# The first two tiles in quarters, half of the ple tiles two output tiles earlier, channel sums by halves and taps moved between heads, in a two-layer retention and convolution trunk on one core

## The reference

```python
for i in range(DEPTH):                       # DEPTH = 2, D_MODEL = 2048
    hn = _rms_norm(x, g_pre[i])
    q, k, v, g_r, a, b, g_c = jnp.split(hn @ w_in[i], SPLITS, axis=-1)    # 7 parts of 1024 columns
    # group A: rotary q, k; retention over 8 heads x 128; norm over each head; * silu(g_r)
    # group B:
    u = a * jax.nn.sigmoid(b)
    c = causal_depthwise_conv(concat(buf0, u), w_dw) + b_dw               # 31 taps, 1024 channels
    c = jax.nn.silu(_layer_norm(c, g_cn, b_cn)) @ w_pw2 + b_pw2
    m = concat(ret_out, c * jax.nn.silu(g_c)) @ w_out
    h = x + _rms_norm(m, g_post[i])
    e = _rms_norm(p[i] @ w_ple[i], g_ple[i])
    x = h + jax.nn.sigmoid(h @ w_ple_gate[i]) * e
```

## Time and profile before

| | us |
|---|---|
| median of 3 runs | 1226.51 (1225.47 to 1227.88) |
| profiled execution, its own time | 1227.37 |
| span of that execution | 1225.4 |
| PE busy | 1197.9 (98%) |
| DVE busy | 926.9 (76%) |
| ACT busy | 604.7 (49%) |
| POOL busy | 94.3 (8%) |

### The profile page before, as it was taken

How to read it: one execution, slowest core, us unless ns; L and a number is a source line. 1 busy time by engine, 2 the same in 40 slices (tenths; PEclk the granted TensorE clock), 3 DMA queues, 4 the chain that set the end, 5 groups by cost and what they waited for, 6 DMA issues and landing times.

```text
span 1225.4 us, 25325 instructions
## 1 busy us (share of the span) xinstructions
PE 1197.9 (98%) x9822; PEld 1192.0 (97%) x9822; DVE 926.9 (76%) x1441; ACT 604.7 (49%) x908; POOL 94.3 (8%) x112
## 2 busy tenths in 40 slices
PE   5999999999999999999999999999999999999998
PEld 5999999999999999999999999999999999999998
DVE  6888899989986644487869879999899764436763
ACT  6433465555556444544544434555555454455351
POOL 0000000000000011311120000000000000123000
PEclk9999999999999999999999999999999999999999
DMA  7655655555545654415565565545555446442362
GB/s 264 212 202 177 207 197 191 192 189 178 205 147 200 224 190 172 170 43 201 190 221 196 195 200 179 207 176 192 192 202 191 157 172 239 173 172 103 136 226 87
DMA packets 42017, 225.69 MB, mean 184 GB/s; under 512 B 6112, under 2 KB 12256, under 8 KB 17888
## 3 DMA queue, kind: packets, MB, share of 16 engines
q1 hardware_dynamic: 27936, 199.37, 45.4%
q10 hardware_dynamic: 14016, 25.42, 6.4%
HBM read 210.97 MB, written 13.81 MB: 183 GB/s over the span
## 4 chain that ended last, share of the span: by engine, by line
PE 85%; DVE 7%; DMA 3%; ACT 2%; issue 2%; ACTq 1%; DVEq 0%; SPq 0%
PE accum_all L446 25%; PE accum_all L447 25%; PE accum_all L448 25%; DMA raw<-w_in 2%; PE ps L512 2%; DVE wlo L994 2%; ACT whi L665 1%; PE accum_all L537 1%; PE accum_all L538 1%; PE accum_all L539 1%; PE ps L462 1%; DMA raw<-w_gate 1%; DVE acc L1301 1%; ACTq L829 1%; DVE tmp L1070 0%
## 5 line engine op out<-in xcount | busy, mean ns | idle before, releaser
L446 PE MATMUL accum_all<-a_hi,whi 128*128 128x264 f32 x2080 | 596.6, 287 | 13.8 <-DVE wlo L994 13.8
L447 PE MATMUL accum_all<-a_lo,whi 128*128 128x264 f32 x2080 | 591.6, 284 | 0.0
L448 PE MATMUL accum_all<-a_hi,wlo 128*128 128x264 f32 x2080 | 591.3, 284 | 0.0
L994 DVE TENSOR_TENSOR wlo<-raw,whi 128x2048 fp32r<-128x2048 f32 x186 | 431.7, 2322 | 194.2 <-ACT whi L665 192.2
L665 ACT ACTIVATE whi<-raw 128x2048 fp32r<-128x2048 f32 x182 | 347.9, 1913 | 168.0 <-DMA raw<-w_in 65.1
L446 PEld LDWEIGHTS accum_all<-a_hi,whi 128*128 128x128 f32 x2080 | 394.2, 190 | 14.5 <-issue 13.8
L447 PEld LDWEIGHTS accum_all<-a_lo,whi 128*128 128x128 f32 x2080 | 394.4, 190 | 0.8
L448 PEld LDWEIGHTS accum_all<-a_hi,wlo 128*128 128x128 f32 x2080 | 392.4, 189 | 0.0
L446 PE MATMUL accum_all<-b_hi,whi 128*128 128x264 f32 x672 | 190.8, 284 | 0.0
L447 PE MATMUL accum_all<-b_lo,whi 128*128 128x264 f32 x672 | 190.4, 283 | 0.0
L448 PE MATMUL accum_all<-b_hi,wlo 128*128 128x264 f32 x672 | 190.3, 283 | 0.0
(11 more groups left out here) (194 smaller groups left out, 1220.7 us busy)
## 6 DMA issues: line engine op xcount, KB each, us to landing
raw<-w_in SPq DMA_DIRECT2D x112, 1024.0 KB, 4.8
raw<-w_out SPq DMA_DIRECT2D x32, 1024.0 KB, 4.8
raw<-w_gate SPq DMA_DIRECT2D x32, 1024.0 KB, 4.8
s_new<-s_ret ACTq DMA_DIRECT2D x16, 512.0 KB, 3.6
...
```

The source lines that it names most:

```text
L446: pe.matmul(accum[bank][:, 0:R], w_hi[:, w:w + P], hi, start=k == 0, stop=False)
L447: pe.matmul(accum[bank][:, 0:R], w_hi[:, w:w + P], lo, start=False, stop=False)
L448: mm = pe.matmul(accum[bank][:, 0:R], w_lo[:, w:w + P], hi, start=False, stop=k == k_tiles - 1)
L994: v.tensor_tensor(wlo[:, slot, :], raw[:, side, :], whi[:, slot, :].bitcast(F32), ALU.subtract).then_inc(s.lo_ready, 1)
```

## The change

It has six parts. (1) **Start:** the slabs of tiles 0 and 1 come in quarters, each group of `x` followed by one quarter of each (SP), and the two tiles are worked side by side, four steps of one and four of the other (`first_two`). Slabs 2 and 3 come into a buffer of their own, `pre`. ACT loads only 16 columns of `vecs`; the rest and the constants come through SP later. ACT has an activation on a spare value first. Tiles 0 and 1 are copied out of PSUM unscaled and scaled when `r_x` is there. The sum of squares is folded to one buffer (`sq_0`) and lies in tile 4, its spreading at step 13 of tile 4. (2) **Taps:** 13 taps leave heads 0 and 1 (5 and 8) and two leave head 6; two more stand in each of the three bodies of the loop over the convolution's tiles, two more in each of heads 2 to 5 and one more in head 7. (3) **Channel sums** in three additions by halves instead of one reduction; `last_values` at step 5 of its tile. (4) **End of a layer:** the first eight ple tiles stand after output tile 11 instead of 13 (`OUT_FIRST` 12), four output tiles behind them. The last four pairs have a second pair of square buffers for two of them and are added by DVE after the last `h_lo`, not by POOL. The sum for `e` lies in gate tile 3 and the spreading in gate tile 4, out of `three_tiles`. (5) DVE's subtractions for gate tiles 4 and 5 come before `gate_tiles`, and ACT rounds the slab of gate tile 6 before the tanh of gate tile 2. (6) The last store goes in parts of 4, 4, 4, 2, 1 and 1 tiles.

```diff
-T_C, T_H, T_G, T_W, T_O, T_EA, T_M, T_EB, T_T, TILES = 0, 16, 48, 56, 64, 78, 86, 88, 96, 112
+T_C, T_H, T_G, T_W, T_O, T_EA, T_M, T_EB, T_T, TILES = 0, 16, 48, 56, 64, 76, 84, 88, 96, 112
-CONV_0, CONV_H0, CONV_C, CONV_1, CONV_2, CONV_3 = 12, 25, 20, 22, 13, 27
+CONV_0, CONV_H0, CONV_C, CONV_1, CONV_2 = 12, 20, 22, 24, 17
-OUT_FIRST, PLE_HALF = 14, 8
+OUT_FIRST, PLE_HALF = 12, 8
+    def e_square(pair):
+        return e_sq[pair // 2 % 2 if 2 * pair >= PLE_HALF else 0][:, pair % 2, :, :]
 # SP
+                for g in range(4):
+                    load_x(g)
+                    for j in range(2):
+                        sp.dma_start(raw[:, j, quarter(g)],
+                                     w_in[rows_of(j), quarter(g)]).then_inc(s.part_in[j][g], 16)
+                sp.wait_ge(s.part_in[0][2], 16)
+                sp.dma_start(pre[:, 0, :], w_in[rows_of(2), :]).then_inc(s.pre_in[0], 16)
+                sp.wait_ge(s.part_in[1][3], 16)
+                sp.dma_start(pre[:, 1, :], w_in[rows_of(3), :]).then_inc(s.pre_in[1], 16)
+                # then the rest of vecs, and consts
-        for i in range(4):
-            sp.wait_ge(s.xnew, KT * (DEPTH - 1) + 4 * i + 4)
+        for t0, t1 in itertools.pairwise((0, 4, 8, 12, 14, 15, KT)):
+            sp.wait_ge(s.xnew, KT * (DEPTH - 1) + t1)
 # PE
-                pe.wait_ge(s.sq0_added, 4)
-                stat_sum(l, ST_X, *(e_buf[:, k, :] for k in range(4)))
+                pe.wait_ge(s.sq0_added, 6)
+                stat_sum(l, ST_X, sq_0[:, 0, :])
+        def first_two():
+            for g, t in itertools.product(range(4), range(2)):
+                ...
+                for k in range(4 * g, 4 * g + 4):
+                    if t == 0:
+                        pe.wait_ge(s.xin_ready, k + 1)
+                    if k == 4 * g and g < 3:
+                        pe.wait_ge(s.first_lo, 2 * g + t + 1)
+                    ...
-            among = {1: {12: mean_over_channels}, 2: {2: last_values},
+            among = {1: {12: mean_over_channels}, 2: {5: last_values},
-                        {5: sum_e, 7: lambda: stat_bcast(l, ST_E)})
-            gemm(l, T_T // BANKS, 3, S_T + 3, S_T + 3, 0, KT, in_b)
+                        {})
+            gemm(l, T_T // BANKS, 3, S_T + 3, S_T + 3, 0, KT, in_b, among={7: sum_e})
+                gemm(l, 1 + T_T // BANKS, j, 4 + S_T + j, S_T + j, 0, KT, in_b,
+                     among={4: lambda: stat_bcast(l, ST_E)} if j == 0 else {})
 # ACT
-        act.dma_start(vecs[:, :, :], vecs_d).then_inc(s.vecs_in, 16)
-        act.dma_start(cst[:, :], consts_d).then_inc(s.consts_in, 16)
+        act.dma_start(vecs[:, 0, V_PRE:V_PRE + KT], vecs_d[:, 0, V_PRE:V_PRE + KT]).then_inc(s.gains_in, 16)
+        nc.scalar.activation(spare, spare, ACT.Copy)
+        for g in range(4):
+            first_x(g)
+            part_hi(0, g)
+            part_hi(1, g)
+        for j in range(2):
+            act.wait_ge(s.tile_done, j + 1)
+            nc.scalar.activation(tmp[j][:, :], accum[j][:, 0:R], ACT.Copy).then_inc(acc_free[j], 1)
-                if pair >= 2:
-                    act.wait_ge(s.esq_used, PLE_HALF * l + pair - 1)
+                if 2 <= pair < PLE_HALF // 2 + 2:
+                    act.wait_ge(s.esq_used, PLE_HALF * l + min(pair - 1, PLE_HALF // 2))
 # DVE
-            head(l, 1, True, False, parts(l, [segment(0, CONV_H0, TAPS), segment(1, CONV_C, TAPS),
-                                              segment(2, CONV_C, TAPS)]))
+            head(l, 1, True, False, parts(l, [segment(0, CONV_H0, TAPS), segment(1, CONV_C, TAPS)]))
...
-            head(l, 6, True, True, parts(l, [segment(3, CONV_C, TAPS), segment(6, CONV_2, CONV_3)]))
-            head(l, 7, True, True, parts(l, [segment(6, CONV_3, TAPS), segment(7, CONV_2, TAPS)]))
+            head(l, 6, True, True, parts(l, [segment(2, CONV_C, TAPS), segment(6, CONV_2, TAPS)]))
+            head(l, 7, True, True, parts(l, [segment(3, CONV_C, TAPS), segment(7, CONV_2, TAPS)]))
+                v.tensor_tensor(half[:, 0:4, :], src[:, 0:4, :], src[:, 4:8, :], ALU.add).then_inc(s.ln_step, 1)
+                # then 2 + 2, then 1 + 1
+            for pair in range(4, PLE_HALF):
+                ...
+                v.tensor_tensor(e_sum[:, :, :], e_sum[:, :, :], e_square(pair), ALU.add).then_inc(s.esq_used, 1)
 # POOL
-            for pair in range(4, PLE_HALF):
-                add_ple(l, pair)
```

312 lines of the change are left out of this document (212 added, 100 removed).

## The result

The changed kernel takes **1210.06 us** (median of 4 runs, 1208.15 to 1212.39), the kernel before on the same chip 1226.96 (4 runs, 1225.47 to 1227.88). The ratio is **0.9863**, 95% interval 0.9847 to 0.9879: 16.9 us faster. The forecast was 1208.1 (18.4 us faster) in a range of 1204 to 1213. The kind came out, and the time lies 2.0 us above the forecast: inside the range, a little above the band that carried the forecast's own chance (1206.7 to 1209.5). The profiled execution of the changed kernel has a time of 1209.43 and a span of 1207.6; before it was 1227.37 and 1225.4. The two traces are 17.9 us apart, against 18.4 in the sum. That the sum comes so near is in part luck: the start gave 3.4 us less than forecast, the norm 1.6 and the ends of the layers 1.2 more.

What follows compares the result with a forecast made beforehand. PE, busy 98% of the span, was taken as the bound; savings of 11.0 + 1.0 + 0.5 + 2.0 + 1.5 + 1.5 + 0.9 = 18.4 us gave 1208.1 us against the median 1226.51, range 1204 to 1213.

Steps and rivals of the forecast that it cites:

- the start: Up to tile 5: first matmul at 7.8 us, tile 5 at 40.4 instead of 51.44, a gain of 11.0 us.
- the norm: Channel sums, both layers: reduction of 4.22 us becomes additions of 2.5, the wait for the mean's subtraction goes; 0.5 us saved.
- the ends of the layers: Without POOL's four additions the `b_lo` waits go: 2.0 us saved in layer 0, 1.5 plus 1.5 of clock in layer 1.
- the sentence on slab 2: Start: slab 2's load lands at about 15.6, is rounded and split by 20, 1.5 us ahead of tile 2 at 21.5.
- the ramp: PE's low clock level after the first matmul, claimed to cost 2.2 us again, as in the trace before.
- rival D: Half clock stays at layer 1's end (+1.5) or follows a wait in start or heads (+3.0): 1209.6 to 1212; chance 0.12.
- Rival C: Start: pieces come slower, 4.0 us a group, the first two tiles end at about 24.7, 3.1 us later: 1211; chance 0.08.
- DVE's lag in layer 0: After the early start: slab 8 ready only 0.9 us ahead of tile 8, heads begin with DVE some 3 us later against PE.
- Rivals A and B: Layer 0: A, DVE's lag exceeds its cover, 1211, chance 0.16; B, no lag, all head waits go, 1205.7, chance 0.14.
- The taps: Heads 0 to 2: waits 2.3 us instead of 1.3 in layer 0, almost none in layer 1; together 1.0 us won.
- The clock's 1.5 at the end of layer 1: End of layer 1: the half clock behind the wait goes too, saving 1.5 us more.
- The last store: End of the kernel: 396 KB less to land after the last issue, 0.9 us saved.

Runs made afterwards that it cites:

- first experiment: Loads of `pre` (slabs 2 and 3) issued without waiting for pieces to land, against the changed kernel: median 1208.95 us, 0.9861 of before, span 1206.5.

## Why the prediction was right, and where it was not

**The start: 11.0 forecast, 7.6 measured.** x's first group landed at 4.6 us for the 4.5 of the sum, and the first matmul came as worked out, at 7.91 for 7.8. Behind it two steps fail.

The larger is the sentence on slab 2, "its load goes out when the third group is there and lands at about 15.6". The load did go out then, at 12.91, but the fourth group, 1040 KB, was still in front of it on the same wires. The third group was complete at 13.6, the fourth at 16.1, and slab 2 followed at 20.45. I had given a load that enters a full queue the time of a load alone. With the issue earliest of all it is 19.7 (first experiment). Cover 1.5 us became a wait of 2.3. The bytes ahead don't explain the whole: a megabyte behind the fourth group took 2.6 us in that experiment and 4.3 here. Loads issued behind slab 2 moved along with it (6.35 MB had gone when it landed, 5.3 had been issued up to and with it); how they share the wires wasn't traced.

The smaller one is the ramp: 2.2 was taken from one trace of before; in the eleven traces of this start the clock rose 3.6 to 6.2 us after the first matmul, and in the profiled run of the changed kernel it rose last. With a first matmul 0.1 later it ended tiles 0 and 1 at 22.4 for the 21.5 forecast, so the ramp cost 0.8 more. The Trainium skill, TensorE: Matmul & The Clock Gate, section What's actually happening, calls this variable from run to run, as rival D said; the traces agree, by 2.6 us. The other part of D's mechanism, a 0.50 stretch behind a wait in the start, came in four of eight traces, at 1.5 us and not at 3.0.

Tile 2 began at 24.86 for 21.5: 0.9 of it for the end of tiles 0 and 1, and 2.5 from start to start for the wait. That is the 3.4 missing at tile 5. Rival C (pieces come slower) has the right time, tile 2 at 24.7, by luck: it wanted PE to run dry inside the first two tiles, and these ended at 22.4 without a wait. The quarters ran at about 400 GB/s, a group in 2.6 us. Several loads of 256 KB in flight together weren't slower than the whole slabs behind them: 397 GB/s at first, 361 to 419 later.

**DVE's lag in layer 0: right.** Slab 8 was ready 0.74 us ahead of tile 8 (forecast 0.9), slab 19 8.1 us ahead of its tile (forecast 0.9 and some 8 won, about 9; before it was 12.1). The waits of heads 0 to 2 were 2.8 us for the 2.3 forecast, on `stack_cols`, `pmat` and `s_new`. That r_x drives them is shown by the earlier sum, 1.1 to 1.4 us for 1.4. Rivals A and B fall. One difference in the working is wrong by itself: 20.6 - 3.4 - 2.2 is 15.0 and not 15.3, and the cover would have been 1.2. The trace has 15.4 from r_x to slab 8, so the slip happened to help. (In the first matmul's bounds, all of the 1.8 us gives 7.2, not 7.0.)

**The taps: the sum right, the share wrong.** -1.6 and +2.6 are the 1.0 forecast. But of that I had the taps win 1.6 in layer 0 and 2.0 in layer 1; undone, they were worth nothing in layer 0 and 1.5 in layer 1. A reading of it that is argued and not shown: in layer 0 DVE is still catching up, and the two taps more in each body of the loop cost there what the heads lose. So the loss of 1.6 us in layer 0 is all from the early start, and the term's sum was right with shares that were not.

**The norm: 2.1 for 0.5.** The durations were right (2.4 for 2.5), the waits were not. The step that failed is the size of "the wait for the mean's subtraction (0.5) goes": it took one place of two. The matmul of the mean waited for `pmat`, behind the reduction on DVE, a row that I left aside as not belonging to the norm:

```profile
PE ps L583 <- DVE pmat L1106: 0.5, 2, 0.3
```

And both are larger than their rows say: from start to start PE lost 0.42 us at each of the two places in layer 0 where the row has 0.26, since a wait's row counts only from the modelled end of the matmul before; up to the next tile's start it is 0.5. The wait that I had in the sum goes by the later place of `last_values`, the one that I left out by the halved sums.

**The end of a layer: 2.0 and 3.0 forecast, 2.7 and 3.5 measured.** The mechanism is shown by moving the additions back: 3.0 and 2.15 us. The forecast had subtracted 0.6 a layer for waits on `e_buf`; measured it is 0.3. The clock's 1.5 at the end of layer 1 came as forecast: no 0.50 is left there. But it is a term that one execution has and another hasn't: the same wait of 1.8 or 1.9 us was followed by a stretch of 0.50 in one of two layers, in the kernel before and in the one with POOL's additions. With the 3.0 at the start the sum counts 4.5 us of it in full; against a faster execution of before the gain is smaller.

**The narrow matmuls.** That the low stretch hung on 24 of them, against 6, I had from layer 1's sum; the experiment with 24 in tile 4 brought it back. Its cost there was 1.4 us, not the 3.0 of before; the trace of the change has neither.

**The last store: 0.95 for 0.9.**
